# Folding the small experts' tiles: transposes and additions on VectorE in place of fold matmuls, and a ninth round that gathers its own rows

## What is computed

```python
def swiglu(x, w1, w3, w2):
    return (jax.nn.silu(x @ w1) * (x @ w3)) @ w2

def moe_ffn(x, router_w, w1, w3, w2):
    logits = (xt @ router_w).astype(F32)
    top_v, top_i = lax.top_k(logits, TOP_K)            # 2 of 8 experts for each token
    top_w = jax.nn.softmax(top_v, axis=-1)
    gates = jnp.sum(jax.nn.one_hot(top_i, N_EXPERTS, dtype=F32) * top_w[..., None], axis=1)
    for e in range(N_EXPERTS):
        y = y + gates[:, e:e + 1].astype(x.dtype) * swiglu(xt, w1[e], w3[e], w2[e])
```

## Time and profile before

| | us |
|---|---|
| median of 3 runs (lowest, highest) | 2330.93 (2329.65, 2336.23) |
| the profiled execution | 2330.9 |
| its span in the profile | 2329.1 |
| TensorE busy (matmuls) | 2288.7, 98% of the span |
| VectorE busy | 1810.3, 78% |
| ScalarE busy | 1383.6, 59% |
| TensorE's share of the chain that ended last | 88% |
| VectorE's share of it | 8% |
| expert stage, steps 0 to 8 | 436.0 to 1418.6 |

### The profile page before, as it was taken

How to read it: one execution, slowest core, us unless ns; L and a number is a source line. 1 busy time by engine, 2 the same in 40 slices (tenths; PEclk the granted TensorE clock), 3 DMA queues, 4 the chain that set the end, 5 groups by cost and what they waited for, 6 DMA issues and landing times.

```text
span 2329.1 us, 29393 instructions
## 1 busy us (share of the span) xinstructions
PE 2288.7 (98%) x11211; PEld 1899.5 (82%) x11211; DVE 1810.3 (78%) x2342; ACT 1383.6 (59%) x1588; POOL 31.7 (1%) x44
## 2 busy tenths in 40 slices
PE   9999999999999999999999998999999999999998
PEld 7788887888888888787888877888888888888887
DVE  4865467989867687899899998899765569987655
ACT  4444444578755666788878874565544435654543
POOL 0000000000000000000000000000000000000000
PEclk9999999999999999999999999999999999999999
DMA  8366654699967799899999995644566565455663
GB/s 279 114 210 188 186 162 158 261 326 407 376 230 269 269 323 344 321 409 412 409 374 408 413 413 202 192 138 152 183 190 190 181 203 163 118 180 172 198 187 122
DMA packets 198508, 584.20 MB, mean 251 GB/s; under 512 B 17259, under 2 KB 26615, under 8 KB 183640
## 3 DMA queue, kind: packets, MB, share of 16 engines
q1 hardware_dynamic: 196060, 573.97, 70.1%
q0 software_dynamic: 1872, 6.82, 0.9%
q10 hardware_dynamic: 428, 1.45, 0.2%
HBM read 580.07 MB, written 2.12 MB: 250 GB/s over the span
## 4 chain that ended last, share of the span: by engine, by line
PE 88%; DVE 8%; ACT 1%; issue 1%; DMA 1%; DVEq 0%; POOL 0%; POOLq 0%; ACTq 0%; SPq 0%
PE tile L1005 19%; PE tile L1007 19%; PE tile L1006 19%; PE tile L1506 5%; PE tile L1507 5%; PE aux L1128 3%; DVE units_parts L2495 3%; PE aux L1492 2%; PE aux L1005 2%; PE aux L1006 2%; PE aux L1007 2%; PE aux L1507 1%; PE aux L1506 1%; PE aux L1419 1%; PE aux L1782 1%
## 5 line engine op out<-in xcount | busy, mean ns | idle before, releaser
L2495 DVE TENSOR_TENSOR units_parts<-units,high 128x1024 fp32r<-128x1024 f32 (+3 forms) x339 | 482.5, 1441 | 93.4 <-ACT high L1910 91.1
L1006 PE MATMUL tile<-units_parts,acts 128*128 128x512 f32 (+2 forms) x1344 | 515.0, 383 | 0.0
L1910 ACT ACTIVATE high<-units 128x1024 fp32r<-128x1024 f32 (+3 forms) x339 | 412.2, 1235 | 153.2 <-DMA units<-in_w_in 40.9
L1005 PE MATMUL tile<-high,acts 128*128 128x512 f32 (+2 forms) x1012 | 401.8, 397 | 6.5 <-DVE units_parts L2495 3.9
L1007 PE MATMUL tile<-high,acts 128*128 128x512 f32 (+2 forms) x1012 | 389.6, 385 | 0.0
L1006 PEld LDWEIGHTS tile<-units_parts,acts 128*128 128x128 f32 x1344 | 254.3, 189 | 47.1 <-issue 2.2
L1005 PEld LDWEIGHTS tile<-high,acts 128*128 128x128 f32 x1012 | 191.3, 189 | 44.9 <-DVE units_parts L2495 5.9
L1007 PEld LDWEIGHTS tile<-high,acts 128*128 128x128 f32 x1012 | 190.9, 189 | 38.5
L1006 PE MATMUL tile<-units_parts,zbuf_parts 128*128 128x512 f32 x328 | 127.6, 389 | 0.0
L1506 PE MATMUL tile<-high,params_parts 128*128 128x512 f32 x276 | 109.0, 395 | 0.0
L1507 PE MATMUL tile<-units_parts,params_parts 128*128 128x512 f32 x276 | 107.7, 390 | 0.0
(11 more groups left out here) (554 smaller groups left out, 5201.0 us busy)
## 6 DMA issues: line engine op xcount, KB each, us to landing
units<-in_moe_w SPq DMA_DIRECT2D x156, 1024.0 KB, 8.0
units<-in_w_in SPq DMA_DIRECT2D x134, 512.0 KB, 4.0
units<-in_w_ff SPq DMA_DIRECT2D x128, 512.0 KB, 3.7
q_buf<-in_moe_w SPq DMA_DIRECT2D x39, 1024.0 KB, 8.5
k_buf<-in_moe_w SPq DMA_DIRECT2D x39, 1024.0 KB, 8.2
nat<-in_moe_w SPq DMA_DIRECT2D x39, 1024.0 KB, 8.7
bias<-in_moe_w SPq DMA_DIRECT2D x39, 1024.0 KB, 9.0
units<-in_ffn_w SPq DMA_DIRECT2D x48, 512.0 KB, 3.7
```

The lines of the kernel that those rows point to most:

```text
L1005: nc.tensor.matmul(bank, lhs[0], high, start=start, stop=False)
L1006: nc.tensor.matmul(bank, lhs[0], low, start=False, stop=False)
L1910: nc.scalar.activation(high_slot(SG[0], n) if wide_ else high_slot(SG[0], n)[:, 0:cols], halves(weights) if wide_ else weights[:, 0:cols], ...
L2495: V.tensor_tensor(low, weights, high, ALU.subtract).then_inc(SG[0].low_ready, 1)
```

## The change

- In few rounds and for the 64 further rows of round 2, `turn_raw` replaces the fold matmuls: 4 transposes into one spare bank for the first matrix and 4 into the other for the second, 8 in all and two banks instead of one. VectorE adds the halves with two `tensor_reduce` (`add_halves`), each reading 512 elements from PSUM, and frees the banks with them. ScalarE then applies the silu in SBUF (`silu_added`), VectorE multiplies in SBUF.
- The tiles of a pair no longer stand together behind unit 9, 17 or 25, but one behind i % 8 = 1 and one behind i % 8 = 2 (`added_after`). In round 2 the tile moves from i % 4 = 1 to 2, the raw copy of the first matrix with it.
- Round 7 no longer gathers for a possible ninth round: in step 8 the choice of rows, the 8 gathers and their copies go, and a conditional round gathers its rows itself before it begins. The scatters of step 8 move from k = 2, 3 to 4, 6.
- In step 0 the rows for round 1 are chosen behind unit 15 instead of 17. `fold` and its making go.

The core of the diff:

```diff
-BACK_SCATTER, BACK_CHOOSE, BACK_GATHER = (2, 3), 2, (4, 5, 6, 7, 8, 9, 10, 11)
+BACK_SCATTER = (4, 6)
...
 def gathers(r):
-    return r <= LARGE or few(r) and r < ROUNDS - 1
+    return r <= LARGE or few(r) and r != N_EXP - 1
...
 def gathered_by(r):
-    return [r + 1, r + 2] if LARGE < r < N_EXP - 1 and gathers(r) else [r + 1] if gathers(r) else []
+    if not gathers(r):
+        return []
+    return [r] if r >= N_EXP else [r + 1] if r <= LARGE else [r + 1, r + 2]
...
-    return [i // 4 - 2, i // 4 - 1] if i >= 9 and i % 8 == 1 else []
+    return [i // 4 - 2, i // 4 - 1] if not few(r) and i >= 9 and i % 8 == 1 else []
...
+def added_after(r, i):
+
+    if r == LARGE:
+        return [i // 4 - 1] if i >= 6 and i % 4 == 2 else []
+    return [i // 4 - 2 + i % 8 - 1] if few(r) and i >= 9 and i % 8 in (1, 2) else []
...
+def tail_added_at(r):
+
+    return TAIL_AT + (r == LARGE) if adds_up(r) else None
...
-                        if few(r) or r == LARGE:
-                            raws = 2 * (t + 1 if r == LARGE else min(2 * (t // 2 + 1), MOE_TILES))
-                            pe.wait_ge(raw_ready, 2 * MOE_TILES * few_before(r) + raws)
-                            bank = spare_bank("folded", r, t)
-                            for m in range(2):
-                                for c in range(4):
-                                    at = m * 4 * FEW + c * FEW
-                                    mm = nc.tensor.matmul(bank[:, at:at + FEW], raw_of(r, t, m)[:, c * P:(c + 1) * P],
-                                                          fold[:, :], start=True, stop=True)
+                    def turn_raw(r, t):
+
+                        raws_of(r, t)
+                        for m in range(2):
+                            bank = spare_bank("raw", r, t, m)
+                            for c in range(4):
+                                at = slice(c * P, (c + 1) * P)
+                                mm = nc.tensor.transpose(bank[:, at], raw_of(r, t, m)[:, at], ident)
                             mm.then_inc(spare_full, 1)
...
                             for t in turned_after(r, i):
                                 turn_tile(r, t)
+                            for t in added_after(r, i):
+                                turn_raw(r, t)
                             if i in GATHER_AT and gathers_within(r):
                                 gather(r, GATHER_AT.index(i))
...
-                            if k in BACK_GATHER and gathers(r):
-                                gather(r, BACK_GATHER.index(k))
...
                         else:
+                            for k in range(8):
+                                gather(s - 1, k)
                             first_matrices(s - 1, None, s - 2)
...
+                    def silu_added(r, t):
+
+                        n = spare_at["raw", r, t, 0]
+                        act.wait_ge(spare_evac[n % 2], n // 2 + 1)
+                        nc.scalar.activation(product_of(r, t)[0], product_of(r, t)[0], ACT.Silu).then_inc(few_silu, 1)
...
+            def add_halves(r, t):
+
+                banks = [spare_in("raw", r, t, m) for m in range(2)]
+                for (bank, evacuated_), dst in zip(banks, product_of(r, t)):
+                    V.tensor_reduce(dst, bank[:, :].rearrange("p (c i n) -> p c n i", c=4, i=2), AX.X,
+                                    ALU.add).then_inc(evacuated_, 1)
+                n = spare_at["raw", r, t, 1]
+                dve.wait_ge(spare_evac[n % 2], n // 2 + 1)
+                dve.wait_ge(few_silu, C.folded.take() + 1)
+                silu, linear = product_of(r, t)
+                V.tensor_tensor(silu, silu, linear, ALU.mult).then_inc(few_added, 1)
...
-                    if i == CHOOSE_AT + (4 if r == 0 else 0) and gathers_within(r):
+                    if i == CHOOSE_AT + (2 if r == 0 else 0) and gathers_within(r):
...
-                    if k == BACK_CHOOSE and gathers(r):
-                        choose(gathered_lots(r), rank)
```

More of the change, by code:

```diff
@@ L497, in build @@
             order_id = sb("order_id", [P, N_EXP], U32, where=one)
-            fold = sb("fold", [P, FEW], where=one)
         squares = gbuf[:, 1024:2048].rearrange("p (u d) -> p u d", u=HEADS1 * TB)
@@ L1594, in first_matrices @@
                             if i == 0:
-                                for q in range(r):
+                                for q in range(r + 1):
                                     if r in gathered_by(q):
@@ L1603, in first_matrices @@
                                 turn_tile(back, LAST_TILE)
+                            if back is not None and i == tail_added_at(back):
+                                turn_raw(back, LAST_TILE)
                             if i in scatter_at(r) and late is not None:
@@ L2174, in first_matrices @@
                                 tile_in(back, LAST_TILE)
-                            if i == TAIL_AT + 2 and back is not None and (few(back) or back == LARGE):
+                            if back is not None and i == tail_added_at(back):
+                                silu_added(back, LAST_TILE)
+                            if i == tail_low_at(back):
                                 high_few(back, LAST_TILE)
@@ L2233, in expert @@
                             END[0] = C.unit.n + MOE_UNITS
+                            for k in range(8):
+                                gathered_in(s - 1, k)
                             first_matrices(s - 1, None, s - 2)
@@ L2958, in find_order @@
                 V.tensor_copy(by_round[:, :, 0:1], by_expert[:, :, 0:1])
-                V.tensor_tensor(fold[:, :], ident[:, 0:FEW], ident[:, FEW:P], ALU.add)
                 step(V.max(sorted_keys, order_keys))
@@ L3112, in first_matrices @@
                         tile_in(back, LAST_TILE)
-                    if i == TAIL_AT + 2 and back is not None and (few(back) or back == LARGE):
+                    if back is not None and i == tail_added_at(back):
+                        add_halves(back, LAST_TILE)
+                    if i == tail_low_at(back):
                         low_few(back, LAST_TILE)
@@ L3118, in first_matrices @@
                         tile_in(r, t)
+                    for t in added_after(r, i):
+                        add_halves(r, t)
                     if few(r):
```

55 lines of the change are left out of this document (30 added, 25 removed).

## The result

The changed kernel takes 2381.66 us (median of 4 runs, 2380.86 to 2388.26) against 2333.01 of the kernel before in the same series: ratio 1.0216, 95% interval 1.0198 to 1.0234. It is slower, as forecast, but by 48.6 us instead of 23, and above the range. Its profiled span is 2379.4 us.

What follows compares the result with a forecast made beforehand. TensorE alone was taken to bound steps 2 and 3; in steps 1, 5 and 7 TensorE, VectorE and DMA end together. 22.1 + 4.5 - 1.8 - 3 + 1 = +22.8 us gave 2354 us, range 2332 to 2368.

Steps and rivals of the forecast that it cites:

- In steps 1 and 5 the wait lies inside the VectorE count.: Gathers behind a second tile in steps 1 and 5: TensorE's wait there adds nothing beyond VectorE's +6.6 and +7.0 us.
- its sum for VectorE: Small steps 1, 5, 7: busy time plus 7.7 us of reductions, six holes of 1.25, 1.9 with gathers; +22.1 us together.
- TensorE should catch up: End of steps 1 and 5: TensorE trails VectorE by its folds and regains some 2.5 us.
- The clock's term: Steps 2 and 3: two of five gather waits bring 3.4 us at 1.2 GHz, half lost; 3.4 us, ends 0 to 8.5.
- Rival (c): The clock falls at every wait, also in steps 1 and 5: 5.1 and 6.8 us more, 2366 us; chance 15%.
- The waits of steps 2 and 3: TensorE's gathers wait for VectorE's reduction: three times 2.25 us in step 2, twice 3.3 in step 3; 13.4 us.
- The holes of 1.23 us: VectorE waits for ScalarE's next cast at each tile, six in a small step: 1.25 us each, from 0 to 2.3.
- Step 7: Small step without gathers: VectorE's 100.0 us grow to 115.2, so +8.5 us against 106.5.
- steps 4 and 6: TensorE stays the bound and saves by transposes replacing folds: -1.8 us together.
- step 0: Rows chosen two units earlier; the gather's wait of 1.63 us and its clock stretch go: -3 us (0 to -4).
- step 8: Gather matmuls go and the scatter moves, but VectorE gets 1.28 + 1.25 us and loses 0.47: +1 us (-4 to +2).
- rival (a): TensorE's gain comes through: reductions fit VectorE's idle time in small steps, gathers don't wait; 2310 us, chance 7%.

Runs made afterwards that it cites:

- e6: Changed kernel plus matmuls with overwritten results between the halves' transposes of tiles 3 and 5 in rounds 1, 3 and 5, filling TensorE's wait; 2367.6 us, ratio 1.0148.
- e1: Changed kernel with the gathers of rounds 1 to 5 moved away from the second tile of a pair; 2349.7 us, ratio 1.0069 to the kernel before.
- e7: Changed kernel with the edits of e1 and e4 together; 2314.2 us, ratio 0.9922 to the kernel before.
- e9: e7 with each reduction done twice, the first result never read; 2342.0 us, ratio 1.0025 to the kernel before.
- e11: e7 with the small rounds choosing rows two units earlier and gathering at 13 to 16 and 20 to 23; 2311.0 us, ratio 0.9912 to the kernel before.
- e4: Changed kernel with silu and product of each tile one unit later, behind the next cast, and some raw copies moved; 2352.4 us, ratio 1.0079 to the kernel before.

## Why the prediction was wrong

**The step that failed** is "In steps 1 and 5 the wait lies inside the VectorE count." It gave no reason; the one meant is that VectorE sets these steps, so a wait of TensorE for VectorE is time in which VectorE works. This holds while the wait lasts. But its length wasn't worked out there; it is 5.5 to 5.8 us, since VectorE has two splits and the hole ahead of the reduction, where step 3 has one split. So both waits were taken at nothing. In that time TensorE loses its place ahead, comes back at the half clock, and ScalarE's copies of gathered rows hold the cast for which VectorE then waits.

In the prediction's own terms: its sum for VectorE gave these two steps 9.4 us of holes each, and took off 2.5 us each that TensorE should catch up at the step's end, a term with no row behind it. Measured are 16.1 and 14.6 us of idle time of VectorE, and nothing was caught up. Together with 1.3 us more of busy time these make the missing 18.2 us. By the runs, step 1's +16.6 us come apart so: 122.6 with all; 117.6 without the half clock (e6); 111.7 with the gathers apart (e1); 106.0 without the holes too (e7), which is the length of before. That is 5.0 + 5.9 + 5.7. For step 5 the same row reads 3.2 + 5.8 + 7.3, from 125.6 to 109.3. The shares depend on the order in which the causes are taken away, and e1 still holds a wait of 3.3 us and 3.4 us at the half clock in each. The prediction had +6.6 and +7.0; the missing 18 us of its total are these.

**The clock's term was mis-sized.** "I count two for the five waits, 3.4 us; none or five are the ends (0 to 8.5)". Steps 2 and 3 have 3.4 + 13.7 = 17.1 us at the lower level where the prediction had two stretches of 3.4. Some 1.9 us of the 17.1 lie within the waits of step 3, and half of the other 15.2, 7.6 us, is what can be lost. Filling the waits of step 3 gave back 5.4 us there, and the half clock that went from step 2, where nothing was filled, 1.5 us: 6.9 us, twice the term. I had taken a stretch of 3.4 us from the earlier trace rows; at the waits of step 3 they last 6.8 us. The waits themselves make 14.2 us instead of 13.4. So steps 2 and 3 came to +10.9 instead of +4.5, and 2 us of this are not accounted for. Rival (c), the clock at every wait, had 15.3 us for the clock in all nine steps, and e6 gives 15.2. Its size was right, its count wasn't: in step 2 only one of three waits of 2.3 to 2.4 us has a stretch, in steps 1, 3 and 5 the stretches are longer. Its 2366 was still too low, since it kept the step that failed.

**What was right.** The waits of steps 2 and 3 (2.25 and 3.3 us predicted, 2.3 to 2.4 and 3.4 to 3.8 measured), from counting units and durations along three engines. The holes of 1.23 us: in step 7 at four tiles, with 1.71 at the fifth. Step 7: +8.5 predicted, +8.0 measured; steps 4 and 6: -1.8, and -1.8; step 0: -3, and -2.3; step 8: +1, and +2.1. The transposes of one pass each: 8 of them take 1.04 us in a row, and steps 4 and 6 got their 0.9 us.

**The count for VectorE was right as a sum and wrong in its parts.** With the gathers apart steps 1, 5 and 7 stand at +5.7, +6.2 and +7.9 us, near the predicted +6.6, +7.0 and +8.5. But this is not 7.7 us of reductions and 7.5 of holes, each of which could be had back: without the holes (e7) nothing is left of it, and the reductions cost nothing; the next 5.4 us of reductions within a step (e9) cost 4 to 5.5. So VectorE's idle time of before had room for the reductions, as rival (a) said, once the handshake doesn't waste it. Rival (a)'s 2310 us is where e11 ended, with three edits more.

**The reduction.** The Trainium skill, in VectorE: DVE Perf Modes, section Rules for kernel authors, speaks against a reduction on the hot path. The rows show 0.684 us for one that reads 512 elements from PSUM, the price of the addition of 512 in the earlier trace rows. The formula in that page's section on the TRN2 errata gives an estimate of 0.66 us; the measurement stands. The form was not what made the change slow. A plain addition of the halves from PSUM was not run.

## What to carry to other kernels

When a cheap step of one engine becomes a dearer one of another, look at what stands next in each queue behind the handshake: here moving the gathers by a few units and letting the next cast go ahead of the silu turned a loss of 2.2% into a gain of 0.8% (e7). A wait for the engine that sets the pace isn't free when the waiting one owes it something soon after; work out the wait's length at each place, and what the waiting engine owes to others when it comes back. Where TensorE has to wait in front of work that is on the path, give the half clock behind it a term of its own.

## What the runs showed of the hardware

TensorE's half clock cost some 15 us of 2382 here: with 4.5 and 2.8 us of matmuls with no use in waits of 5.5 to 5.8 and 3.4 to 3.8 us (e6) it was gone from all nine steps, though 0.9 to 1.4 us of wait were left at each place.

In all runs, each of the 14 waits of 3.3 to 5.8 us in front of a gather came with 3.4 or 6.8 us at 1.2 GHz, which began within the wait or less than 1 us behind it. Shorter waits went either way. Those of 1.86 and 1.95 us in step 3 of e4 have none, one of 1.90 us in step 1 of e7 has 3.4 us, and an equal one in its step 5 none. Of the eight waits of 2.2 to 2.6 us in the stage of the changed kernel four were followed by 3.4 us; of the same eight in e6 none was. What decides it there no run shows.

A reduction that reads 512 elements from PSUM takes 0.68 us, whether it writes 256 values a partition (0.684) or 4 (0.683, e9).
